# Eight heads at once: decay differences and their clamp in a chunked scan

## The reference

```python
def ssd_chunked(xh, dt, a, bm, cm):
    ...
    a_cs = jnp.cumsum(da, axis=-1)
    causal = jnp.tril(jnp.ones((CHUNK, CHUNK), dtype=bool))
    seg = a_cs[..., :, None] - a_cs[..., None, :]
    lmat = jnp.exp(jnp.where(causal, seg, -jnp.inf))
    cb = jnp.einsum("bclgn,bcsgn->bgcls", cc, bc)
    y_diag = jnp.einsum("bgrcls,bcsgrp->bclgrp", cb[:, :, None] * lmat, x_dt)
```

## Time and profile before

| | |
|---|---|
| median of 3 runs | 1285.57 us (1284.64 to 1287.23) |
| profiled execution, its own time | 1287.94 us |
| span of the profile | 1286.2 us |
| mean granted TensorE clock | 0.976 |
| TensorE busy | 1190.0 us, 93% of the span |
| VectorE busy | 492.2 us, 38% |
| ScalarE busy | 246.1 us, 19% |
| GpSimd busy | 198.0 us, 15% |
| scan, four tiles | about 174 to 306 us of the span |

### The profile page before, as it was taken

The page is one execution under the profiler, slowest core; times in us unless marked ns, Lnnn a source line. Parts: engine busy times, 40 slices in busy tenths (PEclk is TensorE's granted clock), DMA queues, the critical chain, the costliest instruction groups (busy, mean ns, idle before and its releaser), DMA issues. The chain is left out here.

```text
span 1286.2 us, 13415 instructions
## 1 busy us (share of the span) xinstructions
PE 1190.0 (93%) x4799; PEld 612.6 (48%) x4799; DVE 492.2 (38%) x1007; ACT 246.1 (19%) x611; POOL 198.0 (15%) x320
## 2 busy tenths in 40 slices
PE   4999999998999999999999999999998998978884
PEld 2435864455554444448854434444443443423331
DVE  5686035654655411113765323222323232212237
ACT  2141122233432100001121212211212121211111
POOL 5000021111002000000271211122111212111101
PEclk9999999999999999999999999999999999989997
DMA  9742242213358952138157999999999999999874
GB/s 302 193 131 65 66 138 93 72 60 132 101 161 291 415 187 88 65 102 332 51 209 293 310 420 421 423 423 422 414 412 400 406 394 402 371 410 407 338 311 177
DMA packets 110985, 334.66 MB, mean 260 GB/s; under 512 B 14356, under 2 KB 67688, under 8 KB 83912
## 3 DMA queue, kind: packets, MB, share of 16 engines
q1 hardware_dynamic: 87824, 269.37, 54.7%
q0 software_dynamic: 18400, 47.10, 10.2%
q10 hardware_dynamic: 4696, 17.35, 3.3%
HBM read 314.49 MB, written 38.35 MB: 274 GB/s over the span
## 5 line engine op out<-in xcount | busy, mean ns | idle before, releaser
L1841 PE MATMUL ps<-gu_hi,xsT 128*64 128x512 f32 (+1 forms) x704 | 245.6, 623 | 24.9 <-DMA gu_hi<-in_exp_w_up_dram 10.3
L1841 PE MATMUL ps<-gu_lo,xsT 128*64 128x512 f32 (+1 forms) x320 | 148.0, 617 | 10.9 <-issue 6.7
L1841 PEld LDWEIGHTS ps<-gu_hi,xsT 128*64 128x64 f32 (+1 forms) x704 | 84.8, 156 | 136.6 <-issue 134.5
L1362 DVE SCALAR_TENSOR_TENSOR hid<-ps,wgt,gated 128x256 f32<-128x256 f32 x42 | 20.3, 484 | 306.6 <-ACT gated L940 306.6
L1849 PE MATMUL ps<-dn_hi,hidT 128*64 128x512 f32 (+1 forms) x352 | 120.6, 601 | 1.3 <-DVE hn L1358 1.1
L1488 PE MATMUL ps<-n1T,ring 128*128 128x512 f32 x256 | 111.9, 593 | 0.0
L1718 PE MATMUL ps<-n1T,ring 128*128 128x512 f32 x256 | 110.9, 592 | 0.7 <-ACT attT L880 0.7
L705 POOL DMA_INDIRECT expert_rows<-hn,meta x40 | 40.0, 1001 | 395.7 <-DVE hn L1358 352.6
L1358 DVE TENSOR_TENSOR hn<-ps,g_row 128x1024 f32<-128x1024 f32 x42 | 51.4, 1225 | 92.2 <-PE ps L1849 92.0
L1841 PEld LDWEIGHTS ps<-gu_lo,xsT 128*64 128x64 f32 (+1 forms) x320 | 51.4, 166 | 62.4 <-issue 62.0
L940 ACT ACTIVATE gated<-ps 128x256 f32<-128x256 f32 x42 | 16.1, 384 | 332.9 <-PE ps L1841 332.9
(11 more groups left out here) (336 smaller groups left out, 1353.9 us busy)
## 6 DMA issues: line engine op xcount, KB each, us to landing
gu_hi<-in_exp_w_gate_dram SPq DMA_DIRECT2D x44, 1024.0 KB, 16.0
gu_hi<-in_exp_w_up_dram SPq DMA_DIRECT2D x44, 1024.0 KB, 30.4
dn_hi<-in_exp_w_down_dram SPq DMA_DIRECT2D x44, 1024.0 KB, 27.6
ring<-in_w_in_dram SPq DMA_DIRECT2D x21, 1024.0 KB, 5.7
gu_lo<-in_exp_w_gate_dram SPq DMA_DIRECT2D x20, 1024.0 KB
gu_lo<-in_exp_w_up_dram SPq DMA_DIRECT2D x20, 1024.0 KB
dn_lo<-in_exp_w_down_dram SPq DMA_DIRECT2D x20, 1024.0 KB
h<-in_ada_w_dram POOLq DMA_DIRECT2D x32, 512.0 KB, 5.4
```

Source lines behind the costliest of these rows:

```text
L1841: ins = pe.matmul(ps[rows, 2 + b, :], xsT[:, b, k, rows], gu(s)[:, :, k, :], start=(k == 0), stop=(k == KC - 1))
```

## The change

For each group of eight heads, eight instructions that subtract one per-partition scalar and clamp at zero become two wide ones: a subtraction of two tensors, of which the second is read through `over`, and a clamp at zero in place. Between the two is a wait of VectorE on its own semaphore.

```diff
                 for g in range(GROUPS):
-                    for hh in range(HG):
-                        hd = HG * g + hh
-                        ins = dve.tensor_scalar(seg[:, hd, :], decay[:, hd, :],
-                                                exarg[:, hd:hd + 1], 0.0, ALU.subtract, ALU.min)
-                    ins.then_inc(seg_done, 1)
+                    hs = slice(HG * g, HG * g + HG)
+                    chain(dve.tensor_tensor(seg[:, hs, :], decay[:, hs, :], over(exarg[:, hs], P), ALU.subtract))
+                    dve.tensor_scalar(seg[:, hs, :], seg[:, hs, :], 0.0, None, ALU.min).then_inc(seg_done, 1)
                 for g in range(GROUPS):
                     dve.wait_ge(decay_done, 2 * t + g + 1)
```

## The result

| | before | after |
|---|---|---|
| median of 20 runs | 1285.58 us (1283.92 to 1287.32) | 1288.59 us (1286.62 to 1290.77) |
| profiled execution, its own time | 1287.94 us | 1289.56 us |
| span of the profile | 1286.2 us | 1287.8 us |
| mean granted TensorE clock | 0.976 | 0.978 |
| VectorE instructions | 1007 | 959 |

The ratio after to before is 1.0022, 95% interval 1.0015 to 1.0029: 2.8 us slower by the ratio, 3.0 by the medians, 1.9 to 3.7 by the interval. 48 instructions fewer, and a slower kernel. The predicted time was 1287.2 us, for a loss of 1.6.

What follows compares the result with a forecast made beforehand. TensorE's stream was taken to bound the kernel to about 730 us, then the transfers. Tiles 1 to 3 add 0.65 + 0.65 + 0.60 = 1.9 us, 1.25 if slow stretches stay put; middle +1.6 gives 1287.2 us, range 1284.6 to 1290.0.

Steps and rivals of the forecast that it cites:

- Where the kernel is bound: TensorE's stream carries the time to about 730 us; a scan delay moves everything behind it by the same amount.
- The tile that has cover: Tile 0 of the scan: 2.6 us of TensorE's fill matmuls hide the 0.65 us delay.
- The price of the pair: VectorE in the scan: a group costs 1.86 us instead of 1.56, so 0.60 us more a tile.
- The holds behind GpSimd: First subtraction held until L603 ends; 0.60 us lost if L609 goes next, 0.71 if the subtraction does; 0.65 taken, tiles 0-2.
- The rival of an unheld subtraction: In the scan, GpSimd does not hold the subtraction: together 4.1 us faster, 1281.5 us; chance 0.07.
- TensorE's waits: Ahead of the 64 matmuls: 3.7, 3.7 and 2.5 us in tiles 1 to 3, none in tile 0.
- The clock gives a part back: Tiles 1 and 2: if slow stretches stay put, later resumption spends less work at half clock, 0.33 us back in tile 1.
- The rival of an extra slow stretch: A longer TensorE wait in the scan brings one more half-clock stretch: loss 3.3 us, 1288.9 us; chance 0.16.

Runs made afterwards that it cites:

- late products: GpSimd's two products moved behind the product with `cb`: kernel before 1274.52 us, changed kernel 1276.31, against 1285.76 for the unmodified kernel before.
- The larger delay: Changed kernel with two more clamps per group in tiles 1 to 3: 1298.78 us, ratio 1.0104 to the kernel before; with filled waits 1291.92.
- filled waits: Unread matmuls added in TensorE's scan waits: kernel before 1281.16 us, changed kernel 1283.10, against 1285.70 for the unmodified kernel before.

## Why the prediction was right or wrong

**Where the kernel is bound: right.** The waits ahead of the 64 matmuls in tiles 1 to 3 are the place. The tile that has cover costs nothing, and a delay in the others passes through once: 8.8 us by the medians for 8.7 in the trace, with the clock held, and the part behind the scan is no longer than before.

**The price of the pair: right.** 0.60 us a tile was forecast, 0.58 measured without GpSimd beside it. The clamp, which had no row of its own, took 0.69 us for an estimated 0.68. The estimate from the cycle table of the Trainium skill ("VectorE: DVE Perf Modes", section on the TRN2 errata), 1.4 us a tile, is more than twice the measurement, mostly because the narrow instructions cost 0.195 us each here and not 0.127.

**The holds behind GpSimd: right.** The first subtraction was held to 2.92 us (2.9 forecast), L609 gave way to it, and the clamp then waited for L609. I had 0.71 us for this order (by its own terms, 218.0 + 0.60 + 1.26 + 0.60 - 219.79, it is 0.67), and 0.57 came out, since the clamp was held 1.58 us (2.27 - 0.69) and not the 1.8 that I had put down for L609. The rival of an unheld subtraction, worth 4.1 us to the other side, is refuted by the trace and by the kernels with late products.

**TensorE's waits: right.** 3.7, 3.7 and 2.5 us forecast, 3.65, 3.65 and 2.56 measured; the sum is 1.8 us where I had 1.9.

**The clock: the term that was off.** "The clock gives a part back" took 0 to 0.65 us off, for a middle of 1.6. The measured loss is 2.8 to 3.0 us (1.9 to 3.7). The delay itself is 1.8 us by the traces and 1.9 with the clock held, and it passes through once. So about 1 us came on top of the delay where I had taken 0.3 off.

The reasoning took one execution's slow stretches as if they stayed where they were. They don't. Already in the trace of the kernel before, tile 2 does not look the same as tile 1, though I wrote that it does: in tile 1 the clock fell while TensorE waited, in tile 2 it was at 1.00 to 254.8 us and at 0.50 from there, just after TensorE had resumed at 254.74. Tile 3 has a stretch in the kernel before, and has none behind the same wait in the kernel with the change in tile 0 alone. And the execution that I read was not a typical one: with 1287.94 us it lies above all 20 timed runs of the kernel before (1283.92 to 1287.32). That it had more or costlier slow stretches than most is likely, but not shown.

The profiled pair alone would have confirmed me, and that would have been luck. It is 1.6 us apart, as forecast (1289.56 us, where I had 1289.5): the two steps behind the waits (64 matmuls and the product with the state) took 16.8 us before and 15.8 after, so that a part did come back, but `turn_u(3)` took 1.97 instead of 1.17, and 0.5 us of the difference arose before the scan's first 64 matmuls, ahead of the changed code. Over 20 runs the balance went the other way. The larger delay points there too: 10.2 us above the changed kernel unfilled, 8.8 filled, though this difference is within the scatter. The rival of an extra slow stretch gave 3.3 us, and the medians lie near it, but no trace here shows that stretch: the profiled pair has the same time at half clock.

What is shown is that holding the clock by filled waits gains 4.5 us in the kernel before and 5.5 in the changed one (1288.59 to 1283.10). That the difference of these two is what the change lost beyond its delay is argued: it is 1 us with an uncertainty as large, and no trace shows where that microsecond lies.

**The numbers.** The time lies in the range of 1284.6 to 1290.0 and at the very end of the forecast's own, 1285.8 to 1288.6 (median 1288.59). The loss is nearly twice the forecast 1.6 us. I gave 0.64 to no difference, drawn at 0.2%, and 0.27 to slower; the ratio, 1.0022, lies on the border of the two, and its interval, 1.0015 to 1.0029, shuts out a loss of nothing.

## What to carry to other kernels

Count an instruction at its distance to the next one, not at its duration: narrow ones that overlap are cheaper than they look, and a fused one with two operations per pass can beat two wide ones that pass twice. Before VectorE is tuned, look at what GpSimd does beside it: taking two products out of the way was worth about four times what this change cost. A wait of TensorE costs its length, and then what the clock takes from the work behind it; the second part can't be read from one execution, but its size (here 4.5 us) can be measured by filling the waits.

## What the runs showed of the hardware

Sixteen VectorE instructions of 128 columns run 0.196 us apart though each is recorded at 0.275. A fp32 product of VectorE with one operand read through a broadcast was held as long as a GpSimd product ran (2.92 us for 1.22), and held GpSimd in turn (2.88 us for 1.90); the two engines took turns in every tile of the changed kernel's trace. Of TensorE's clock, a wait of 3.1 us in tile 1 was followed by half clock in the kernel before, and so was one of 3.2 us at `turn_u(3)`; in the kernel before with late products a wait of the same 3.2 us there was followed by none. The wait of 1.9 us in tile 3 was followed by half clock in the kernel before and by full clock in the one with the change in tile 0 alone. The Trainium skill, "TensorE: Matmul & The Clock Gate", part on the clock gate, says that what watches TensorE's activity runs free of the kernel, so that the place of a transition varies from run to run. These traces agree with it: behind the waits of tiles 1 to 3, which are as long in both, the 64 matmuls took 3.40, 3.63 and 2.81 us in the kernel before and 2.93, 2.86 and 2.27 in the one with the change in tile 0 alone.
